# The way from the first layer norm to the first bunch of experts, rearranged

## The reference

```
x = layer_norm(ALPHA * x + y, ln1_g, ln1_b)
g_logits = x @ w_rg + b_rg                 # 4 groups
grp = argmax(g_logits);  p_grp = softmax(g_logits)[grp]
e_logits = (x @ w_re[grp]) + b_re[grp]     # 8 experts of the group
top_val, top_idx = top_k(e_logits, 2)
gate = softmax(top_val) * p_grp
out[token] += gate * (silu(x @ w_gate[e]) * (x @ w_up[e])) @ w_down[e]   # for its two experts
x = layer_norm(ALPHA * x + out, ln2_g, ln2_b)
```

## Time and profile before

| what | us |
|---|---|
| median of 3 runs | 768.28 (767.44 to 771.92) |
| profiled execution, device time | 766.16 |
| its span, first to last instruction | 764.4 |
| outside the span | 1.76 |
| PE busy in the span | 681.9 (89%) |
| DVE busy | 368.5 (48%) |
| ACT busy | 324.1 (42%) |

### The profile page before, as it was taken

How to read it: one execution, slowest core, us unless ns; L and a number is a source line. 1 busy time by engine, 2 the same in 40 slices (tenths; PEclk the granted TensorE clock), 3 DMA queues, 4 the chain that set the end, 5 groups by cost and what they waited for, 6 DMA issues and landing times.

```text
span 764.4 us, 11653 instructions
## 1 busy us (share of the span) xinstructions
PE 681.9 (89%) x4580; PEld 524.3 (69%) x4582; DVE 368.5 (48%) x813; ACT 324.1 (42%) x759; POOL 16.8 (2%) x31
## 2 busy tenths in 40 slices
PE   6989999996599999697887789999979999999986
PEld 4968998695363555253452378888859898888876
DVE  1633657445431232021110376678775566787743
ACT  2555665421000112120110243578875545788742
POOL 6001000000000000000000000000000000000000
PEclk9999999998599999899999899999999999999999
DMA  9967331498667999999999919007263080073301
GB/s 281 339 196 245 111 111 56 127 358 313 247 269 255 416 407 415 413 411 415 410 415 415 322 61 299 29 1 248 83 220 111 1 258 19 1 223 109 111 1 56
DMA packets 82328, 167.80 MB, mean 220 GB/s; under 512 B 4238, under 2 KB 59264, under 8 KB 78176
## 3 DMA queue, kind: packets, MB, share of 16 engines
q1 hardware_dynamic: 79984, 160.88, 58.1%
q0 software_dynamic: 2160, 6.07, 2.4%
q10 hardware_dynamic: 128, 0.08, 0.0%
HBM read 165.93 MB, written 1.07 MB: 218 GB/s over the span
## 4 chain that ended last, share of the span: by engine, by line
PE 70%; SPq 13%; ACT 5%; DVE 5%; DMA 5%; issue 2%; ACTq 0%; DVEq 0%
PE psum L850 13%; PE psum L852 11%; PE psum L851 11%; SPq L740 9%; PE psum L1204 5%; PE psum L1246 4%; PE psum L893 3%; PE psum L1144 3%; PE psum L1191 2%; DMA ring<-in_w_expert_up_dram 2%; PE psum L1260 2%; SPq L685 2%; DMA ring<-in_w_in_dram 2%; PE psum L1103 2%; PE psum L1232 1%
## 5 line engine op out<-in xcount | busy, mean ns | idle before, releaser
L850 PE MATMUL psum<-a_high,w_high 128*128 128x256 f32 x512 | 150.9, 295 | 2.1 <-ACT q_c L1471 1.3
L851 PE MATMUL psum<-x_low,w_high 128*128 128x256 f32 x512 | 144.6, 283 | 0.0
L852 PE MATMUL psum<-a_high,w_low 128*128 128x256 f32 x512 | 144.6, 283 | 0.0
L2186 DVE TENSOR_TENSOR w_low<-ring,w_high 128x1024 fp32r<-128x1024 f32 (+1 forms) x79 | 111.2, 1422 | 25.1 <-ACT w_high L1571 25.1
L850 PEld LDWEIGHTS psum<-a_high,w_high 128*128 128x128 f32 x512 | 97.7, 191 | 13.9 <-issue 4.7
L1571 ACT ACTIVATE w_high<-ring 128x1024 fp32r<-128x1024 f32 (+1 forms) x79 | 95.9, 1219 | 10.7 <-DMA ring<-in_w_in_dram 7.4
L851 PEld LDWEIGHTS psum<-x_low,w_high 128*128 128x128 f32 x512 | 97.8, 191 | 0.4
L852 PEld LDWEIGHTS psum<-a_high,w_low 128*128 128x128 f32 x512 | 97.8, 191 | 0.0
L1246 PE MATMUL psum<-ring,q_c 128*32 128x512 f32 x368 | 60.7, 654 | 14.6 <-DMA ring<-in_w_expert_up_dram 10.0
L850 PE MATMUL psum<-w_high,a_high 128*128 128x256 f32 x240 | 69.6, 290 | 0.0
L851 PE MATMUL psum<-w_low,a_high 128*128 128x256 f32 x240 | 68.5, 285 | 0.0
(11 more groups left out here) (334 smaller groups left out, 1168.4 us busy)
## 6 DMA issues: line engine op xcount, KB each, us to landing
ring<-in_w_in_dram SPq DMA_DIRECT2D x36, 1024.0 KB, 8.6
ring<-in_w_expert_gate_dram SPq DMA_DIRECT2D x46, 512.0 KB, 14.5
ring<-in_w_expert_up_dram SPq DMA_DIRECT2D x46, 512.0 KB, 15.6
ring<-in_w_expert_down_dram SPq DMA_DIRECT2D x22, 1024.0 KB, 17.4
ring<-in_w_out_dram SPq DMA_DIRECT2D x12, 1024.0 KB, 5.2
ring<-in_w_mem_kv_dram SPq DMA_DIRECT2D x4, 1024.0 KB, 16.8
mixT<-in_w_expert_down_dram SPq DMA_DIRECT2D x3, 1024.0 KB, 18.7
xT<-in_w_expert_down_dram SPq DMA_DIRECT2D x3, 1024.0 KB, 20.6
```

The costliest lines, as they stand in the source:

```text
L850: pe.matmul(dst, left[0], right[0], start=first, stop=False)
L851: pe.matmul(dst, left[0], right[1], start=False, stop=False)
L852: return pe.matmul(dst, left[1], right[0], start=False, stop=last)
L2186: dve.tensor_tensor(w_l, raw_of(n), as_f32(w_h), ALU.subtract).then_inc(lows, 1)
```

## The change

It does five things.

1. x is transposed by token halves: four `x1t` jobs (tt, half of the features), of four chunks each. Those of half 0 wait only for `ln_done` 1. Two `logit` jobs stand behind them, one for each half.
2. The logits are computed with tokens as rows: 128 tokens of `xT` are the stationary operand, the 36 router columns the moving one. Job `logitT`, its bias add across partitions and its copy go. The bias is loaded as a row spread over all partitions (`route_row`).
3. `first_of` uses one scalar_tensor_tensor for each half in place of two linked instructions; the groups that were not chosen are shut off with one small instruction.
4. VectorE starts on `rank` after three of its five products (semaphore `ranked`); the list lengths go to bank 3 and are reduced afterwards. The product with `chosen` is dropped, since the added -1024 alone makes the other places unequal.
5. The selection matrix is signalled by `located`, before the gate weights are worked out (`gates_of`) and before the weighted matrix (`weigh`), which now signals `placed`. TensorE waits for `placed` only ahead of `turn_weighed`.

```diff
     jobs = [("y1", s, tt) for s, tt in Y_ORDER]
-    jobs += [("x1t", k) for k in range(4)] + [("logit",), ("logitT",), ("rank",)]
+    for tt in range(2):
+        jobs += [("x1t", tt, 0), ("x1t", tt, 1), ("logit", tt)]
+    jobs += [("rank",)]
...
-                pool.dma_start(route_b[0:GROUPS, :], ins["b_route_group"].rearrange("o g -> g o")).then_inc(small_in, 16)
+                pool.dma_start(route_row[:, 0:GROUPS], ins["b_route_group"][0].partition_broadcast(P)
+                               ).then_inc(small_in, 16)
...
                 elif kind == "x1t":
-                    pe.wait_ge(ln_done, 2)
-                    mm = turn4(dst, x4, job[1])
+                    tt, half = job[1:]
+                    pe.wait_ge(ln_done, tt + 1)
+                    for c in range(4):
+                        mm = pe.transpose(dst[:, P * c:P * c + P], x4[:, tt, 4 * half + c, :], ident)
                 elif kind == "logit":
-                    from_act(("x1t", 3))
+                    tt = job[1]
                     pe.wait_ge(router_in, 16 * (1 + GROUPS))
                     for k in range(KC):
-                        mm = pe.matmul(dst[0:GROUPS + EXPERTS, 0:T], router[:, k, :], xT3[:, k, :],
+                        if k % 4 == 0:
+                            from_act(("x1t", tt, k // 4))
+                        mm = pe.matmul(dst[:, 0:GROUPS + EXPERTS], xT3[:, k, P * tt:P * tt + P], router[:, k, :],
                                        start=(k == 0), stop=(k == KC - 1))
...
-                    pe.matmul(dst[:, e:2 * e], ones, chosen3[:, 0, :], start=False, stop=True)
-                    pe.matmul(dst[:, 2 * e:3 * e], ones, chosen3[:, 0, :], start=True, stop=False)
-                    mm = pe.matmul(dst[:, 2 * e:3 * e], ones, chosen3[:, 1, :], start=False, stop=True)
+                    pe.matmul(dst[:, e:2 * e], ones, chosen3[:, 0, :], start=False, stop=True).then_inc(ranked, 1)
+                    for tt in range(2):
+                        mm = pe.matmul(bank(3)[:, 0:e], ones, chosen3[:, tt, :], start=(tt == 0), stop=(tt == 1))
...
-                pe.wait_ge(p_dve, taken(JOB[("rank",)]))
                 pe.wait_ge(setup, 2)
-                pe.wait_ge(placed, 1)
+                pe.wait_ge(located, 1)
                 gather_half(0)
+                pe.wait_ge(p_dve, taken(JOB[("rank",)]))
                 for b in range(BUNCHES):
                     gate_up(b, 0)
                     if b == 0:
                         gather_half(1)
+                        pe.wait_ge(placed, 1)
                         turn_weighed()
...
-                link(dve.tensor_tensor(score3, values3, wide(best), ALU.is_equal))
-                link(dve.tensor_tensor(score3, score3, order, ALU.mult))
+                for tt in range(2):
+                    op = dve.scalar_tensor_tensor(score3[:, tt], values3[:, tt], best[:, tt:tt + 1], order,
+                                                  ALU.is_equal, ALU.mult)
+                link(op)
...
+            def locate_first(src):
+
+                dve.wait_ge(ranked, 1)
+                link(dve.tensor_tensor(rank, src[:, 0:2 * EXPERTS], e_sc, ALU.add))
+                for tt in range(2):
+                    op = located_in(0, None, tt)
+                op.then_inc(located, 1)
...
             def experts():
-                places(0, None, link)
+                gates_of()
+                dve.wait_ge(located, 1)
+                weigh(0)
                 back_copy(0, backs[0])
```

More of the change, by code:

```diff
@@ L170, in all_loaded @@
     return 16 * sum(PIECES.get(ITEMS[m], 1) for m in range(n + 1) if slot_of(m) == slot_of(n))
-TAKEN_BY_DVE = ("bias", "xt2", "y1", "logit", "logitT", "rank", "swap")
+TAKEN_BY_DVE = ("bias", "xt2", "y1", "logit", "rank", "swap")
 Y_ORDER = ((0, 0), (0, 1), (1, 0), (1, 1), (2, 0), (3, 0), (2, 1), (3, 1))
@@ L725, in free_for_experts @@
                 elif k == X_T:
-                    sp.wait_ge(p_ready, JOB[("logit",)] + 1)
+                    sp.wait_ge(p_ready, JOB[("logit", 1)] + 1)
                 else:
@@ L1408, in take @@
                     op = act.activation(vecs[:, :], src[:, 0:41], ACT.Copy)
-                elif kind in ("xt", "x1t"):
+                elif kind == "xt":
                     k = job[1]
-                    to = xT_1 if kind == "xt" else xT3
-                    op = act.activation(to[:, 2 * k:2 * k + 2, :], src.rearrange("p (c t) -> p c t", c=2), ACT.Copy)
+                    op = act.activation(xT_1[:, 2 * k:2 * k + 2, :], src.rearrange("p (c t) -> p c t", c=2), ACT.Copy)
+                elif kind == "x1t":
+                    tt, half = job[1:]
+                    op = act.activation(xT3[:, 4 * half:4 * half + 4, P * tt:P * tt + P],
+                                        src.rearrange("p (c t) -> p c t", c=4), ACT.Copy)
                 elif kind == "cnat":
@@ L1711, in _ @@
                         layer_stats(0, job[2])
-                    elif job[0] == "logitT":
+                    elif job == ("logit", 1):
                         act.wait_ge(route_dif, 1)
@@ L2033, in route @@
                                   ).then_inc(route_dif, 1)
-                m4 = e_m.rearrange("p (t g e) -> p t g e", t=2, g=GROUPS)
-                s4 = e_sc.rearrange("p (t g e) -> p t g e", t=2, g=GROUPS)
-                one = g_one.rearrange("p (t g) -> p t g", t=2)
-                for tt in range(2):
-                    ow = one[:, tt, :].unsqueeze(2).to_broadcast([P, GROUPS, PER_GROUP])
-                    ev = e3[:, tt, :].rearrange("p (g e) -> p g e", g=GROUPS)
-                    dve.tensor_tensor(m4[:, tt], ev, ow, ALU.mult)
-                    link(dve.tensor_scalar(s4[:, tt], ow, -NEG, NEG, ALU.mult, ALU.add))
-                link(dve.tensor_tensor(e_m, e_m, e_sc, ALU.add))
+                link(op)
                 m3 = e_m.rearrange("p (t n) -> p t n", t=2)
@@ L2049, in route, with gates_of @@
                 dve.tensor_tensor(e_t, e_mx2, e_mx1, ALU.subtract).then_inc(route_m, 1)
+                dve.wait_ge(chosen_done, 1)
+                link(dve.tensor_scalar(e_sc, chosen, -ABSENT, ABSENT, ALU.mult, ALU.add))
+            def locate_first(src):
+                dve.wait_ge(ranked, 1)
+                link(dve.tensor_tensor(rank, src[:, 0:2 * EXPERTS], e_sc, ALU.add))
+                for tt in range(2):
+                    op = located_in(0, None, tt)
+                op.then_inc(located, 1)
+            def gates_of():
+                m3 = e_m.rearrange("p (t n) -> p t n", t=2)
                 dve.wait_ge(route_exp, 1)
@@ L2284, in _ @@
                         lambda_sums()
+                    if job == ("rank",):
+                        locate_first(bank(6 + j % 2))
                     if BY_DVE[j]:
@@ L2296, in _ @@
                         scaled(0, job[2])
-                    if job == ("logitT",):
-                        route()
+                    if job == ("x1t", 0, 0):
+                        dve.memset(ones, 1.0)
+                    if job == ("logit", 1):
+                        choose()
                     if job[0] == "tile2" and job[2] in GATE_TILES:
```

68 lines of the change are left out of this document (33 added, 35 removed).

## The result

| | before | after |
|---|---|---|
| median of the compared executions | 767.37 us (763.19 to 772.12, 20 runs) | 763.65 us (759.38 to 768.29, 20 runs) |
| profiled execution: time, span, mean granted clock | 766.16 us, 764.4 us, 0.962 | 759.58 us, 757.7 us, 0.961 |

The ratio of the times is 0.9945, 95% interval 0.9924 to 0.9965: the kernel is faster by 3.7 us, where 8.8 were forecast. The time itself lies just inside the stated range of 755.0 to 764.0. Two things stand out. The profiled execution of after lies at the fast end of its own runs, and those runs spread over 9 us. Both turn out to matter.

The account below looks back on a forecast made before the run. The prediction took the experts' weight stream, started by TensorE's first gather, as the bound. Gains of 3.5 + 1.0 + 2.1 + 2.2 = 8.8 us from 767.2 gave 758.4 us, range 755.0 to 764.0.

Parts of the forecast that it names:

- what bounds the kernel: Experts' weight stream: its start sets its end, so each microsecond saved up to the first gather starts it one earlier.
- the case that I had left open: Already issued DMA: shifts up to 8 us cost nothing; 9 to 11 would at worst delay the first megabyte.
- Parts 1 and 2: Transposes and logits by halves: logits ready at 188.2 instead of 191.70, a gain of 3.5 us.
- the row on the 16 transposes: Trace row from 182.39 to 186.15: clock back at 186.75 after transposes only, so transposes count as work for the clock.
- The case that I forecast: Clock low for `logit` 0, back about 185.1, full for `logit` 1; logits gain 3.5 us; forecast's chance 0.48.
- Part 3, the choice: Logits to rank products: 5.20 becomes 4.2, a gain of 1.0 us, with 0.17 from each expert search.
- Parts 4 and 5: Rank to gather: 4.43 becomes 2.35, a gain of 2.1 us; gate weights and weighted matrix behind it cost nothing.
- The first gate_up: TensorE works 6.5 us without pause, so the first gate_up runs at full clock: 3.64 instead of 5.82, 2.2 us gained.
- the first gate_up stays slow: Rival: the gather's long weight loads leave the first gate_up slow; gain 6.6 us, 760.6 us; chance 0.08.
- The rest: Bias loads, job numbers, banks and VectorE's extra waits: nothing else moved, 0 us, with 0.5 in the range.
- gain is lost behind the stream: Rival: second block is TensorE-bound and its clock falls may shift; half the gain gone, 763 us; chance 0.12.

Follow-up runs that it names:

- without the branch: Code of the never-entered further expert rounds removed on four engines: changed kernel 757.50 us (0.9870), kernel before 764.36 us (0.9959).
- the repeat: The changed kernel measured again with no edit: 762.65 us, ratio 0.9941 to the kernel before.
- parts 1 and 2 alone: Kernel before with only the transposes and logits by token halves; choice, rank and places as before: 765.51 us, ratio 0.9977.
- 128 idle instructions: Changed kernel with 128 TensorE waits for a semaphore long set, 32 in each of bunches 4 to 7: 763.57 us, ratio 0.9942.
- late parts: Kernel before with only parts 3 to 5 (choice, rank, places), transposes and logits as before: 762.45 us, ratio 0.9936; second profile 764.78 us.
- two padded: Changed kernel with 228 or 128 TensorE instructions added that wait for a semaphore long set: 759.95 us (0.9899) and 763.57 us (0.9942).
- filled: Changed kernel with nine unused 512-column products of zeros on TensorE between the logits and rank: 762.54 us, ratio 0.9942.
- branch moved: TensorE's branch over the further rounds put ahead of the last bunch's `add_back`: changed kernel 760.35 us (0.9908), kernel before 766.28 us (1.0009).
- the two kernels given the 28 alone: 28 TensorE waits for a semaphore long set added in bunch 4: kernel before 769.05 us (1.0031); kernel with only parts 3 to 5, 769.67 us (single execution).
- 12 instructions: Kernel before with 12 TensorE waiting instructions added in bunch 4: 771.66 us in a single execution.

## Why the prediction was wrong

The gain was real, 3.7 us where 8.8 were forecast. About 2 of the missing 5 are in the front, 3 behind the stream. By the prediction's own steps:

**Read rightly: what bounds the kernel.** The stream hands the shift on whole, 184.7 to 185.4 us in every profile. Transfers that were already issued did not come late for a shift of 9.8 us, the case that I had left open. The issues forecast for 203 and 227 came at 202.28 and 226.35, but that match is luck: 1.7 us of it were won ahead of the change, and the other two profiles of the changed kernel have 205.90 and 229.96, 204.43 and 228.49.

**Parts 1 and 2, right in size, wrong in the clock.** 3.3 us against 3.5, in the first profile. The clock did not come back at 185.1. Windows of after:

```profile
180.00:197.50 17.50, 12.50 (x58) 11.98 (x57) 8.08 (x41) 1.61 (x4) 0.00 (x0) 0.51 1.02 393
197.50:203.00 5.50, 4.76 (x38) 2.13 (x37) 0.00 (x0) 0.60 (x1) 0.29 (x1) 1.00 0.61 242
```

`logit` 1 took 3.54 at the low clock where 1.8 and 0.2 were forecast. What saved the sum is `logit` 0, 2.28 instead of 3.4, since part of it still ran at the full clock: +1.5 and -1.1. That these two errors nearly cancel is luck. The start of `logit` 0, 3.2 us behind the last `y1` (3.3 forecast), and the 1.75 between the two jobs (1.85) came as worked out. I took the row on the 16 transposes that were followed by a rise, against the rule of the Trainium skill that I had cited ("TensorE: Matmul & The Clock Gate", Part 4: PE-mode transpose). The traces of the kernel before speak against that rule: in the one without the branch the clock also came back, between 184.5 and 185.0 us, while TensorE had done nothing but transposes since 181.43. Those of the changed kernel don't decide it: here eight transposes stood between two jobs of narrow products and the clock stayed low, and in two of three profiles rank products and gather, which are no transposes, left it low as well. Nor do narrow products always leave it low: `logit` 0 ran at the full clock and `logit` 1 at the low one in the repeat and in the profile without the branch, and both at the full clock in parts 1 and 2 alone. Where the clock falls on this way differs from one execution to the next. The case that I forecast, low for `logit` 0 and full for `logit` 1, is in none of the nine profiles with parts 1 and 2.

**Part 3, the choice, mis-sized.** 0.6 against 1.0. The pair of `scalar_tensor_tensor` takes 0.42 to 0.43 (two instructions of 0.2) where I had 0.34, so that each of the two expert searches gains 0.09 less. That is half of the missing 0.4; the group search, for which I had 0.12, gained nothing (0.98 before, 0.99 after), and the memset gave less than its 0.1.

**Parts 4 and 5, right.** 2.0 against 2.1. The gate weights behind it cost nothing that the chain shows.

**The first gate_up, the step that failed in the front.** "Now it works ... some 6.5 us without a pause, longer than the 4.4 us after which the clock came back" held in the first profile of after (3.64), and not in the two others of the same program (5.58 and 5.33). Of the five variants of the whole change one has 3.64 (128 idle instructions) and four 5.33 to 6.09. Fronts of the changed program were 50.63, 51.90 and 53.42, against 58.72, 58.72 and 58.66 before: a gain of 5.2 to 8.1, on average 6.7. That is close to what the two kernels differ by without the branch (6.9). So with the whole change the rival "the first gate_up stays slow" is the usual case, and the full clock the lucky one; where it is slow, 1.7 to 1.9 of the 2.2 us are gone, which with the terms above makes the 2 us that the front lacks. Why it is the usual case is open: with parts 3 to 5 alone the same rank products and gather were followed by a gate_up of 3.64 in all three profiles.

**"The rest. ... nothing else is moved. I put 0": the step that failed behind the front.** TensorE passes a branch after the last bunch. Its pause of 3 us, mostly with a stretch of low clock behind it, makes the join 33.7 to 35.9 us in place of 31.1 to 32.1, and the tail mostly 346.0 to 347.0 in place of 340.3 to 343.2. It comes and goes by the execution: in one of three profiles of before, in one of two of the late parts, and in all ten profiles with 28 or more added instructions ahead of the branch (three of after, two padded, filled, branch moved, parts 1 and 2, and the two kernels given the 28 alone). Two more, of before with the branch moved and with 12 instructions, have a shorter one of 1.4 and 1.5. The profiles give the size: a join of 34.6 to 34.9 in all three of after against 32.1 in two of three of before, so 2 to 3 us of the 6.7 are lost here. The medians fit that without proving it: the branch costs 2.9 us in before and 5.2 to 6.1 in after, and the 28 instructions make before 769.05 - 767.31 = 1.7 slower with the branch and 0.3 without, differences within the noise of one another. This was the rival "gain is lost behind the stream", with the right place and size (763), but for another reason than the clock alone; I gave it 0.12.

That it is the branch is shown: none of the three profiles without it has a pause, both kernels are faster without it, clear of the noise, and in the changed kernel the pause moves with it. The removal took it off four engines at once; that TensorE's own branch makes the pause rests on the move, which touched TensorE alone, and so on one profile. That it is the fetch of instructions is argued. The Trainium skill, "Runtime: NRT & Kernel Launch", Instruction fetch mechanics, says that a taken branch to a target outside the blocks already held makes the engine wait for a transfer of its page; the trace agrees as far as it goes, with 3 us of "issue" while the DMA engines are 0.83 busy (425.4 to 428.5 us of after). No run separates this from another cost of the branch. What stays open is why the same program has it in one execution and not in the next, how often, and why added instructions make it so much more frequent; the padding to 256 instructions in all did not bring it to none.

**Two versions have a lower median than both kernels** and keep all of the function: the changed kernel with the branch moved ahead of the last `add_back`, 760.35 (0.9908 [0.9874, 0.9942]), and the one with 228 idle instructions, 759.95 (0.9899 [0.9865, 0.9934]). Against the kernel before that is clear; against the changed kernel (0.9945 [0.9924, 0.9965]) it is not, since the intervals overlap. I would take the first; why the second is faster, if it is, is not settled. The limit is the one without the branch, 757.50.

## What to carry to other kernels

A gain at the start of a DMA-bound stream arrives whole at its end, but the next join may be late for another reason: follow the chain past the stream, look there for runtime branches, and try to put one where its engine waits several microseconds anyway (here only a wait of 0.9 us was tried, and it hid a third). When the runs of a kernel spread over 1% and one profile sits at their edge, take two or three profiles before a term of one of them is believed; the terms here that were luck are 1.7 us ahead of the change, 2 us in gate_up, 2 in `logit`, 3 us at the branch, and up to 4 in the second block. An experiment that removes the suspect in both kernels (6.9 us apart without the branch, 3.7 with it) tells more than one that removes it in one.

## What the runs showed of the hardware

- A runtime branch that is passed over goes with a pause of 2.9 to 4.5 us of "issue" on TensorE in 12 of the 17 profiles that have it, a shorter one of 1.4 or 1.5 in two, and none in three, among them other executions of the same programs. Its presence alone is worth 2.9 to 6 us of a 765 us kernel. Whether the spread of the times comes with it is not shown: 9 us with it in both kernels, and 2 (of six executions), 5 and 7.5 without it.
- The granted clock can stay at 0.5 (1.2 GHz) through long stretches in which the records call PE busy: from 180.0 to 197.5 us of after it was 0.51 with 12.5 us busy, with products of 36 and 32 moving columns, transposes, and a gather whose weights are read with a stride. Nine wide products before the rank products brought it to 1.00 at 193.0 us; it fell at 196.4, in a wait of 0.56 us, and stayed low through the gather. That narrow work is the reason is not shown: in parts 1 and 2 alone both jobs with 36 columns ran at the full clock.
- Two unlinked `scalar_tensor_tensor` of 128x32, with a factor that is read for each partition, take 0.42 to 0.43 us on VectorE, against the 0.34 that the rows of before suggested and the 0.29 that two `tensor_tensor` of the same shape took in the same trace.
